# Joined FFN up steps: eight products of 512 columns first, then eight of 256

## The reference

```
u = _causal_dwconv(x @ w_up[i], ffn_conv_w[i]) + ffn_conv_b[i]
val, gate = u[..., :D_FF], u[..., D_FF:]
x = _layer_norm(ALPHA * x + (jax.nn.silu(gate) * val) @ w_down[i], ln2_g[i], ln2_b[i])
```

## Time and profile before

| | |
|---|---|
| median of 3 runs | 708.16 us (706.64 to 710.5) |
| profiled execution, its own time | 708.14 us |
| span of its trace | 706.2 us |
| TensorE busy | 689.5 us, 98% of the span |
| DVE busy | 519.5 us, 74% |
| ACT busy | 370.0 us, 52% |
| HBM read | 115.19 MB, 165 GB/s over the span |
| mean granted TensorE clock | 0.983 |

### The profile page before, as it was taken

One profiled execution on the slowest core, in us unless ns is written; L12 is line 12 of the kernel. 1 busy time (PEld: TensorE's weight loads), 2 busy tenths in 40 slices (PEclk: granted clock), 3 DMA queues, 4 the chain that ended last, 5 costly groups with the idle time before them and its releaser, 6 DMA issues.

```text
span 706.2 us, 11208 instructions
## 1 busy us (share of the span) xinstructions
PE 689.5 (98%) x4310; PEld 604.1 (86%) x4310; DVE 519.5 (74%) x762; ACT 370.0 (52%) x556; POOL 95.4 (14%) x54
## 2 busy tenths in 40 slices
PE   8999999999999999999999999999999999999995
PEld 5899998877998888888878999988889888888884
DVE  4675768768897777777696466697859977777756
ACT  5664535423776555666356443553248666666630
POOL 0000020221262111110000000204005511111000
PEclk9999999699999999999999999998999999999999
DMA  9971443332765555555338233513357855555301
GB/s 294 318 253 62 151 148 120 120 100 80 261 239 192 195 196 195 197 201 185 122 120 267 91 120 120 176 65 120 120 183 235 294 182 178 179 178 178 119 0 59
DMA packets 87401, 116.81 MB, mean 165 GB/s; under 512 B 5230, under 2 KB 73536, under 8 KB 87360
## 3 DMA queue, kind: packets, MB, share of 16 engines
q1 hardware_dynamic: 85920, 111.85, 47.6%
q10 hardware_dynamic: 1440, 4.39, 1.9%
HBM read 115.19 MB, written 1.05 MB: 165 GB/s over the span
## 4 chain that ended last, share of the span: by engine, by line
PE 92%; DVE 5%; DMA 1%; issue 1%; ACT 1%; SPq 0%; DVEq 0%; ACTq 0%
PE bank L1194 19%; PE bank L1196 18%; PE bank L1195 18%; PE bank L1454 17%; PE bank L1456 9%; PE bank L1279 3%; PE bank L1266 2%; DMA x_tok<-in_x 1%; PE bank L1215 1%; DVE x_tok L970 1%; DVE stats L954 1%; DVE x_tok L952 1%; PE bank L1258 1%; PE bank L1345 1%; DVE ring_lo L308 1%; DVE x_tok L978 1%
## 5 line engine op out<-in xcount | busy, mean ns | idle before, releaser
L308 DVE TENSOR_TENSOR ring_lo<-raw,ring_hi 128x2048 fp32r<-128x2048 f32 x102 | 232.6, 2285 | 23.0 <-ACT ring_hi L304 22.7
L304 ACT ACTIVATE ring_hi<-raw 128x2048 fp32r<-128x2048 f32 x102 | 194.3, 1908 | 13.2 <-DMA raw<-in_w_in 9.3
L1454 PE MATMUL bank<-xx,ring_hi 128*128 128x512 f32 x512 | 181.4, 398 | 0.0
L1456 PE MATMUL bank<-xx,ring_lo 128*128 128x256 f32 x512 | 143.8, 281 | 0.0
L1454 PEld LDWEIGHTS bank<-xx,ring_hi 128*128 128x128 f32 x512 | 96.2, 188 | 23.8
L1456 PEld LDWEIGHTS bank<-xx,ring_lo 128*128 128x128 f32 x512 | 96.7, 189 | 0.6
L721 POOL COPY step_par<-ffn_par 128x16 f32 (+1 forms) x22 | 64.3, 2927 | 221.5 <-DVE work L989 221.5
L1194 PE MATMUL bank<-xx,ring_hi 128*128 128x256 f32 x320 | 92.4, 289 | 0.0
L1195 PE MATMUL bank<-xx,ring_hi 128*128 128x256 f32 x320 | 90.5, 283 | 0.0
L1196 PE MATMUL bank<-xx,ring_lo 128*128 128x256 f32 x320 | 90.5, 283 | 0.0
L1194 PE MATMUL bank<-ring_hi,xx 128*128 128x512 f32 (+1 forms) x224 | 81.5, 364 | 3.8 <-DVE xx L783 3.8
(11 more groups left out here) (186 smaller groups left out, 998.1 us busy)
## 6 DMA issues: line engine op xcount, KB each, us to landing
raw<-in_w_up SPq DMA_DIRECT2D x44, 1024.0 KB, 5.2
raw<-in_w_down SPq DMA_DIRECT2D x22, 1024.0 KB, 5.0
raw<-in_w_in SPq DMA_DIRECT2D x21, 1024.0 KB, 5.2
raw<-in_cmp_w SPq DMA_DIRECT2D x8, 1024.0 KB, 5.9
raw<-in_w_out SPq DMA_DIRECT2D x8, 1024.0 KB, 4.8
qkv<-in_ln_g ACTq DMA_DIRECT2D x4, 512.0 KB, 3.6
qkv<-in_ln_b ACTq DMA_DIRECT2D x4, 512.0 KB, 5.0
raw<-in_w_in SPq DMA_DIRECT2D x2, 512.0 KB, 5.1
```

The lines of the kernel that those rows point to most:

```text
L304: nc.scalar.activation(ring_hi[slot_of(L, u)][:], raw[raw_of(L, u)][:], ACT.Copy).then_inc(hi_done, 1)
L308: eng.tensor_tensor(ring_lo[slot_of(L, u)][:], raw[raw_of(L, u)][:], ring_hi[slot_of(L, u)][:].bitcast(fp32), ALU.subtract).then_inc(split ...
L1454: pe.matmul(dst[:], wh[:, k, P * c:P * (c + 1)], xx[:, k].rearrange("p a n -> p (a n)"), start=k == 0, stop=False)
L1456: ins = pe.matmul(dst[:, 0:SEQ], wl[:, k, P * c:P * (c + 1)], xh[:, k, :], start=False, stop=k == KT - 1)
```

## The change

In each group of a joined step, the loop over `k` with two products in its body becomes two loops: first the eight products of 512 columns, then the eight of 256.

```diff
                             for k in range(KT):
                                 pe.matmul(dst[:], wh[:, k, P * c:P * (c + 1)], xx[:, k].rearrange("p a n -> p (a n)"),
                                           start=k == 0, stop=False)
+                            for k in range(KT):
                                 ins = pe.matmul(dst[:, 0:SEQ], wl[:, k, P * c:P * (c + 1)], xh[:, k, :], start=False,
                                                 stop=k == KT - 1)
```

## The result

The changed kernel takes 703.76 us (median of 22 runs, 701.41 to 708.23), the kernel before 706.62 us in the same series (22 runs, 704.16 to 713.97). The ratio estimated from these runs is 0.9948, with a 95% interval from 0.9930 to 0.9966: faster, by 0.52%. (The plain quotient of the two medians is 0.9960, that of the two means 0.9951; all three lie in the interval.) The forecast was 705.1 against 708.14, which is 0.9957. So the size was nearly right, and the time lies just inside the lower edge of the range (703.7 to 708.6). But I had given "within 0.5%" 0.69 and "faster" only 0.28, and by the estimated ratio faster is what was measured.

The account below looks back on a forecast made before the run. TensorE's own rate alone bounds the joined steps. Alternation and down parts give 3.4 and 1.0 us, handovers and the short first pair take back 1.1 and 0.3: 708.1 - 3.0 = 705.1 us, range 703.7 to 708.6.

Parts of the forecast that it names:

- The sum: Joined step: product rates, four changes of size each way and the down part give 16.60 us, 0.19 us less.
- settled long products: 512-column products well into a run of their own kind, starts 0.2267 us apart.
- A: Joined steps: order does not matter, each product brings its price along, time stays at 708.1 us; chance 0.20.
- B: Joined steps: short products lose their cover for weight loads, 0.13 us more a step, 710.2 us; chance 0.08.
- C: Joined steps: changing size is free, long products settle at once, 16.53 us a step, 704.0 us; chance 0.12.
- handover: Change of size between runs: 0.027 us more from short to long, 0.01 us less back, four each a joined step.
- stray: Whole kernel: a measured time can differ from the worked one by one or two us.

Follow-up runs that it names:

- 16 and 16: Against the kernel before: per weight unit 16 long products of both halves, then their 16 short ones; 703.02 us (5 runs), then 702.50 us (10 runs).
- shifted slice: Against the kernel before: still alternating, but the short product beside the long one of slice k takes slice k + 4; 707.56 us, one run.

## Why the prediction was right and wrong

**What bounds the kernel: right.** TensorE alone sets the pace of the joined steps, before and after, and the products' starts, not their durations, give its rate. That nothing else would wait held too.

**The sum: right for this kernel.** I worked out 16.60 us a step; it is 16.61. Its parts: settled long products 0.227 us (0.2267 taken), eight long ones behind short ones 1.84 us (1.84 taken), settled short ones 0.120 (0.1200), the first interval of a short run 0.007 and the second 0.001 us under that (0.01 taken), the down part 5.46 (5.47). The gain by the trace is 2.8 us, 3.0 were forecast, and the shortest runs at equal clock are 2.9 to 3.0 apart.

**Order has a price.** With the same products a step took 16.79, 16.69, 16.61, 16.59, 16.57 or 16.55 us, by their order alone, up to 1.4% apart. The Trainium skill (TensorE: Matmul & The Clock Gate, Back-to-back issue gap) gives an isolated warm product a gap of N / 2.4 + 2.5 ns for N columns, 216 ns for 512, and says in the same place that in a stream of weight loads and products both set the spacing. These kernels are such streams: a settled product of 512 columns stands 0.2267 us from the next, over that formula, and the formula has no term for the order that the traces show.

**The rivals: refuted.** A and B: long products with xx as their moving side settle at 0.227 us in a run, so the 0.238 that both let them keep was not their own price. The short ones did not pay more than 0.12. C: the handover is not free, since the first eight long products behind short ones take 1.84 us where settled ones take 1.81, and a step is 16.61 us and not 16.53. That the median, 703.76 us, lies beside C's 704.0 is luck: a base of 706.6 us with a gain of 2.9 gives the same time as my base of 708.1 with C's 4.1.

**What failed: the step from the sum to the chances.** "The forecast is 0.43% and so just inside" put 0.69 on the inside of a border that lay 0.5 us from the forecast, while I named strays of one or two us a few sentences before. With a stray of 1.5 us a forecast that lies 0.5 us inside a border ends outside in more than a third of cases (an estimate from these two numbers), before C is added, so 0.28 for "faster" was too low. The term that was mis-sized is the stray: I used it to widen the range and left it out where it decided between "within 0.5%" and "faster". What the runs showed: the steps give 2.8 us, 0.40% of 706.62, on my side of the border; the ratio, 0.52%, came out 0.1% above that, and this part is not in any step. As far as the record shows it lies in the dips of the clock, which the sum put at nothing; why they favoured the changed kernel stays open. The interval, 0.34% to 0.70%, holds the steps, the forecast and the border, so the time came out as "faster" by a hair.

**And the base was mis-sized.** I centred the time on 708.14 us, "the median of the runs". A longer series of before has a median of 706.62, 1.5 us lower, and this is why the median came out at the edge of the range; on the ratio it has no bearing (3.0 of 706.62 is 0.42%). The profiled execution had half clock for 13.5 us in the first layer's attention stage. It stood in the earlier trace rows, the 6 among the nines, where the changed kernel's row has an 8, and I read it as "at full speed in nearly every slice". This digit is 3.5 us of the profiled execution, more than the change is worth, and it differs from run to run. Had I followed it, I would have known that the runs' spread, 706.64 to 710.5, was dips, and that three runs don't say where their median lies.

**The reason: right in its fact, too simple as a law.** That alternating long and short products costs some 0.006 us a pair over settled rates is shown at 256 and, against a settled rate that is an estimate, at 384 columns. That grouping gives it back is true for runs of eight of 512 and 256, and false for runs of eight of 512 and 384. "Handover" as a fixed price fails with runs of two and four. My sum was right because every piece in it was read from a row with the same sizes in the same order, not because the law behind it holds. Why it is so stays open.

## What to carry to other kernels

Take a product's price on TensorE from the distance of starts, in a stretch with the same sizes in the same order; where sizes are mixed, try two or three orders, since the best one can't be worked out from the rates of each size alone. Before you compare two profiles by their spans, compare them ahead of the first changed instruction and look at the clock's row there: here 3.5 us of a difference of 6.7 lay there, and the same program had spans 7.3 us apart. Where a forecast lies nearer to a border than runs stray, no side of it deserves a high chance, however good the sum is.

## What the runs showed of the hardware

A run of one size does not settle at once. Behind eight short products the first eight long ones take 1.84 us instead of 1.81 and are settled after five; behind eight of 384 columns they take 1.85, with no settling within the eight. Mean pairs of a long and a short product, from the lengths of the steps less a down part, are 0.353 us alternating, 0.348 in twos, 0.350 in fours, 0.348 in eights.

The granted clock falls in the attention stage, in both layers of every profile whose windows are shown or named here, but for different times: 0.93, 0.87, 0.80, 0.78, 0.74 and 0.61 were seen as means of the same 26 us. In the kernel before the fall shows in the products of 30 columns, which stand 0.11 us apart at first and 0.21 at the end:

```profile
127.28 0.26 PE L1194 MATMUL bank<-kcTh,qTh 128*128 128x30 f32 x1
127.39 0.26 PE L1195 MATMUL bank<-kcTl,qTh 128*128 128x30 f32 x1
...
129.72 0.38 PE L1194 MATMUL bank<-kcTh,qTh 128*128 128x30 f32 x1
129.93 0.37 PE L1195 MATMUL bank<-kcTl,qTh 128*128 128x30 f32 x1
```

Between a window mean of 0.74 and one of 0.87 in the first layer lie 3.5 us of time (down part 0 at 202.99 and 199.50 us), and between 0.87 and 0.93 almost nothing (199.50 and 199.48 in the kernel with 16 and 16, 199.19 in the one with the shifted slice): with the clock at 0.93 TensorE waits 0.8 us for DVE there (L1345 in its list). Two such stretches explain most of the spread of the changed kernel's timed runs, 701.4 to 708.6 us, since its two profiled executions, of 702.0 and 708.6 us, differ by little else.
